# Reordering the work ahead of the first expert slots and moving the gate1 multiply of the output weights from VectorE to GpSimd

## Chip, cores and metric

The kernel runs on one core of one Trainium2 chip. The metric is the device time of one execution in microseconds. Engines are named as in the profile: PE (TensorE; PEld its weight loads), DVE (VectorE), ACT (ScalarE), POOL (GpSimd), SP (SyncE). A timeline row gives start, duration, engine, line of the kernel, operation, output<-inputs and count; the bracket behind it is the engine's idle time before it and what ended that.

## What is computed

One decoder layer on a sequence of 1024 tokens of width 1024, all in float32. A mixer (causal pooling beside spatial gating) and then a product-key retrieval network over 16384 experts of one neuron each:

```python
mod = silu(c) @ w_ada + b_ada                      # shift1, scale1, gate1, shift2, scale2, gate2
h = rms_norm(x, g_norm1) * (1 + scale1) + shift1
a, u, v = split(h @ w_in)
mixed = concat([pool_mixer(a), spatial_gating(u, v)])
x = x + gate1 * (mixed @ w_out)
h = rms_norm(x, g_norm2) * (1 + scale2) + shift2
q = (h @ w_query).reshape(T, 8 heads, 2, 128)
s_top, i_top = top_k(q . sub_keys, 16)             # two sides of 128 keys for each head
best, sel = top_k(all 16 x 16 sums, 16); gate = softmax(best)
act = gelu(expert_down[idx] . h)                   # 16 experts a head, 128 a token
x = x + gate2 * sum(gate * act * expert_up[idx])
out = rms_norm(x, g_final)
```

## The kernel before

The tokens are cut into 8 tiles of 128. Each tile has 128 slots, 1024 in all; a slot is one expert for each of the 128 partitions. A partition holds a quarter of a token's work, so that a slot fetches 128 rows of 8 KB (down and up row of an expert), 1 MB, with one indirect DMA from POOL's queue into a ring of 7 buffers. In slot g DVE takes the dot product of the row with the token's h (`dot`, L1560), ACT applies Gelu and the gate and builds a diagonal (`expert_weight`, L1130 to L1137), and PE adds the up rows, weighted by that diagonal, into PSUM (`add_expert`, L900). PE's product counts up `s_free`, which lets POOL issue the gather of slot g + 7. A slot of late tiles has 9 buffers.

The work of the eight tiles is laid out by hand: every engine has its own instruction list, made by Python loops, and waits only on semaphores, so an instruction stands behind everything ahead of it on its engine. Between the slot's own steps each engine's loop over `TABLE` carries out steps of four other jobs at fixed slot numbers:

- the mixer of the next tile, 35 steps n, in slot MIX_AT[tile] + n (`mixer`): norm and transposes (0 to 4), projection to v in four steps of two matmuls 128x512 (PROJECT_V, 5 to 8), to a (9 to 12), to u (13 to 20), pooling and gating, the output projection (25 to 32), the residual (34). Tile 1 has its steps below MIX_HEAD ahead of the slots.
- the queries and scores of the next "turn" (two heads of a tile: 4 sides, each a query of 8 matmuls, an ACT copy, a score matmul, an ACT copy), at SIDE_AT. Each side's weights come by a load on SP's queue into three buffers.
- the routing of a turn on DVE, 19 steps from ROUTE_AT (`route_step`): top 16 of each side, of the sums, their indices, softmax weights (the exponential is ACT's, `exp_logits`), then `move_choices` on PE (L889), which spreads the chosen rows and gates over the partitions, and `place_choices` on DVE (L1552), which writes the rows that POOL's gathers read. POOL waits for it at the first slot of each routing (`s_placed`). Routings 0 and 1 are the two heads of turn 0 (slots 0 to 31, four of the one and four of the other in turn), routing 2 is turn 1 (slots 32 to 63).
- spreading h over the partitions (`spread_first_h2`, PE L725, ACT copies L1103), rows of shift2 and scale2, and others. These share one PSUM bank ("wide"), whose uses are put in a fixed order by `wide_bank_uses`; a `moved` use takes the first free pair of slots from ROUTE_AT + 19.

Ahead of the slots stands the head: the adaLN sums of the six parts of w_ada (2 x 2 MB each), the whole mixer of tile 0, the norm of its result (L1328 residual, L1385 to L1412 statistics and scales), routings 0 and 1, part of tile 1's mixer and the four queries of turn 1. Tile 0's mixer multiplies its result by gate1 itself (L1325); for the later tiles w_out is multiplied by gate1 once, in place, in four parts of 128x2048 (`scale_w_out`, L1269, on DVE in slots 3, 6, 9 and 12). SP's queue issues all plain loads in order, those of x for tile 1 (L514) and then of the last w_ada part, GATE2, behind the residual of tile 0. GATE2's sums on PE (L679) must be done before routing 0's last step, since that overwrites their other operand. POOL's list is two memsets, a wait on GATE2's sums, and the gathers.

## Time and profile before

| | us |
|---|---|
| median of 3 runs | 2828.95 (2825.89 to 2829.47) |
| the profiled execution | 2833.91 |
| its span | 2832.1 |
| mean granted TensorE clock | 0.712 |

| | busy us | share | instructions |
|---|---|---|---|
| PE | 1938.6 | 68% | 13316 |
| DVE | 1894.8 | 67% | 4714 |
| ACT | 1210.7 | 43% | 3867 |
| POOL | 1123.1 | 40% | 1030 |

A busy share is a mean over the whole span; the table of stretches further down shows the parts. A DMA share near 1 means that the 16 DMA engines have packets all the time. GB/s is what they moved.

### The profile page before, as it was taken

What the parts mean: (1) busy time and instruction counts of PE and PEld (TensorE: products, weight loads), DVE (VectorE), ACT (ScalarE), POOL (GpSimd) and SP (SyncE); (2) the same over time, 40 slices, a digit from 0 to 9 for tenths busy, and PEclk for the clock granted to TensorE, in tenths of its full rate; (3) what the DMA queues carried; (4) which work ended last, traced back from release to release, by engine and by line L of the source; (5) the groups of instructions that cost most, each with busy time, mean ns of one, the idle gap of its engine ahead of it and who ended that gap; (6) DMA issues with size and microseconds to landing.
All of it is one profiled execution on the core that took longest, in us unless ns stands there. A gap on an engine that the chain in (4) does not pass through costs nothing.

```text
span 2832.1 us, 38640 instructions
## 1 busy us (share of the span) xinstructions
PE 1938.6 (68%) x13316; PEld 893.8 (32%) x13316; DVE 1894.8 (67%) x4714; ACT 1210.7 (43%) x3867; POOL 1123.1 (40%) x1030
## 2 busy tenths in 40 slices
PE   5898898888886566666656666665666666665553
PEld 4555354444442222232323222221322323221110
DVE  5686776785766567677666757677676756676454
ACT  1245445454453344454444434444343544344333
POOL 0044334344443254444444444444444444344342
PEclk9998898899886566665666667665766666576555
DMA  9899999999999999999999999999999999999997
GB/s 404 339 373 403 396 413 417 409 420 420 420 401 397 416 422 421 421 421 421 421 421 421 421 421 419 416 421 421 417 415 421 419 421 416 421 415 421 421 420 294
DMA packets 169221, 1162.38 MB, mean 410 GB/s; under 512 B 19009, under 2 KB 25665, under 8 KB 35778
## 3 DMA queue, kind: packets, MB, share of 16 engines
q0 software_dynamic: 147456, 1073.81, 91.9%
q1 hardware_dynamic: 21570, 86.11, 7.7%
q8 instruction: 106, 1.74, 0.2%
q14 instruction: 89, 0.73, 0.1%
HBM read 1151.97 MB, written 7.86 MB: 410 GB/s over the span
## 4 chain that ended last, share of the span: by engine, by line
DMA 54%; PE 22%; DVE 11%; ACT 6%; issue 3%; SPq 3%; POOL 0%; another core or an unknown queue 0%; DVEq 0%; POOLq 0%; ACTq 0%
DMA work<-experts,expert_rows 41%; DMA more_ring<-experts,expert_rows 8%; PE ps_sum L900 7%; DVE work L1560 5%; PE ps_small L866 5%; PE ps_m L815 4%; DMA work<-w_ada 2%; PE ps_m L759 2%; DMA weights<-experts,expert_rows 1%; ACT diag L1137 1%; ACT weight L1132 1%; DMA vn_u<-x_scratch 1%; PE ps_wide L841 1%; SPq L613 1%; PE ps_m L770 1%
## 5 line engine op out<-in xcount | busy, mean ns | idle before, releaser
L650 POOL DMA_INDIRECT work<-experts,expert_rows x818 | 899.0, 1099 | 1378.7 <-PE ps_sum L900 1225.8
L1560 DVE CUSTOM_DVE_ANT_0 work<-work 128x1024 f32<-128x1024 f32 x818 | 997.5, 1221 | 589.3 <-DMA work<-experts,expert_rows 573.4
L900 PE MATMUL ps_sum<-work,diag 128*32 128x256 f32 x6544 | 717.5, 523 | 674.7 <-ACT diag L1137 653.6
L1130 ACT ACTIVATE act_out<-act_in 128x1 f32<-128x1 f32 x1024 | 207.4, 203 | 1162.8 <-DVE act_in L1560 1141.9
L900 PEld LDWEIGHTS ps_sum<-work,diag 128*32 128x32 f32 x6544 | 150.1, 126 | 1146.5 <-ACT diag L1137 1052.1
L1137 ACT ACTIVATE diag<-const,weight 128x32 f32<-128x32 f32 x1024 | 329.2, 321 | 33.5
L1132 ACT ACTIVATE weight<-gate,act_out 128x1 f32<-128x1 f32 x1024 | 301.6, 295 | 33.3
L866 PE MATMUL ps_small<-h_t,weights 128*128 128x128 f32 x1344 | 291.2, 384 | 0.0
L866 PEld LDWEIGHTS ps_small<-h_t,weights 128*128 128x128 f32 x1344 | 249.3, 278 | 125.7 <-issue 120.4
L1560 DVE CUSTOM_DVE_ANT_0 more_ring<-more_ring,work 128x1024 f32<-128x1024 f32 x122 | 149.1, 1222 | 91.5 <-DMA more_ring<-experts,expert_rows 90.4
L650 POOL DMA_INDIRECT more_ring<-experts,expert_rows x122 | 134.8, 1105 | 180.3 <-PE ps_sum L900 175.5
L841 PE MATMUL ps_wide<-h_cur,const 32*128 32x512 f32 x244 | 191.0, 872 | 0.0
L900 PE MATMUL ps_sum<-more_ring,diag 128*32 128x256 f32 x976 | 108.1, 527 | 85.0 <-ACT diag L1137 84.1
L1560 DVE CUSTOM_DVE_ANT_0 weights<-weights,work 128x1024 f32<-128x1024 f32 x84 | 102.7, 1222 | 67.8 <-DMA weights<-experts,expert_rows 66.3
L1103 ACT COPY work<-ps_wide 128x512 f32<-128x512 f32 x144 | 83.5, 580 | 130.4 <-PE ps_wide L841 107.3
L900 PE MATMUL ps_sum<-weights,diag 128*32 128x256 f32 x672 | 80.1, 564 | 82.3 <-ACT diag L1137 80.2
L650 POOL DMA_INDIRECT weights<-experts,expert_rows x84 | 88.2, 1050 | 120.3 <-PE ps_sum L900 119.1
L815 PE MATMUL ps_m<-weights,h_buf 128*128 128x512 f32 x256 | 124.8, 615 | 0.0
L1110 ACT COPY q_t<-ps_small 128x128 f32<-128x128 f32 x124 | 32.3, 261 | 123.5 <-PE ps_small L866 122.8
L1560 DVE DVE_READ_ACCUMULATOR2_ANT act_in<- 128x1 f32 x1024 | 83.6, 82 | 0.0
L1130 ACT ACT_TABLE_LOAD x59 | 75.7, 1283 | 2.0 <-DVE act_in L1560 0.9
L900 PEld LDWEIGHTS ps_sum<-more_ring,diag 128*32 128x32 f32 x976 | 22.5, 126 | 151.1 <-ACT diag L1137 139.5
(200 smaller groups left out, 1991.1 us busy)
## 6 DMA issues: line engine op xcount, KB each, us to landing
work<-w_ada SPq DMA_DIRECT2D x12, 2048.0 KB, 23.6
work<-sides SPq DMA_DIRECT2D x26, 576.0 KB, 8.4
work<-experts,expert_rows POOLq DMA_INDIRECT x818
weights<-sides SPq DMA_DIRECT2D x16, 576.0 KB
more_sides<-sides SPq DMA_DIRECT2D x12, 576.0 KB
weights<-w_in SPq DMA_DIRECT2D x3, 2048.0 KB, 17.2
x_buf<-x SPq DMA_DIRECT2D x8, 512.0 KB, 11.4
weights<-w_out SPq DMA_DIRECT2D x2, 2048.0 KB, 37.5
```

What stands on the lines that cost most here:

```text
L650: nc.gpsimd.indirect_dma_start(ring[x.ring], None, experts, bass.IndirectOffsetOnAxis(ap=rows_flat[:, x.column:x.column + 1], axis=0),).th ...
L759: last = nc.tensor.matmul(ps_v[:, :], h_t[:, k, :], w_in_sb[:, 0, k, :], start=(k == 0), stop=(k == KC - 1))
L815: last = nc.tensor.matmul(ps_out[half], mixed_t[:, k, :], w_out_sb[:, k, half * HALF:(half + 1) * HALF], start=(part == 0 and i == 0), sto ...
L841: nc.tensor.matmul(ps_wide[:, :], quads[quarter(group), :], source[quarter(group), half * HALF:(half + 1) * HALF], start=True, stop=True). ...
L866: last = nc.tensor.matmul(ps_query(n), w_q[:, k, :], h2_t[:, k, :], start=(k == 0), stop=(k == KC - 1))
L900: last = nc.tensor.matmul(ps_sum[quarter(c), x.group, :], diag[:, x.ring, :], ring[x.ring][:, D + c * QCOLS:D + (c + 1) * QCOLS], start=x. ...
L1103: nc.scalar.copy(h2_spread[k % 2][:, half * HALF:(half + 1) * HALF], ps_wide[:, :]).then_inc(s_wide_sb, 1)
L1110: nc.scalar.copy(q_t[:, n % 2, :], ps_query(n)).then_inc(s_q_sb, 1)
L1130: nc.scalar.activation(act_out[:, s:s + 1], act_in[:, s:s + 1], ACT.Gelu).then_inc(s_gelu, 1)
L1132: nc.scalar.mul(weight[:, s:s + 1], gate_flat[:, x.column:x.column + 1], act_out[:, s:s + 1]).then_inc(s_weight, 1)
L1137: nc.scalar.mul(diag[:, x.ring, :], quad_rows, weight[:, s:s + 1]).then_inc(s_diag, 1)
L1560: nc.vector.tensor_tensor_reduce(down, down, h2_spread[x.segment % 2], 1.0, 0.0, ALU.mult, ALU.add, act_in[:, x.g % TURN:x.g % TURN + 1]). ...
```

## The change

Four things are done.

1. The order of PE's and ACT's lists ahead of the slots. On PE: the first side of turn 1 stands between the two halves of the first spread; the second placement's `move_choices(1)` goes behind the second side, ahead of its score; of tile 1's mixer only steps 0 to 5 stay in the head (MIX_HEAD 6 in place of 9), and the fourth side of turn 1 goes to slots 0 to 4 (SIDE_AT[0]). On ACT: `exp_logits(1)` goes right behind the second spread copy; the copies of h, queries and scores are interleaved to match.
2. Slot numbers: tile 1's mixer steps come three slots later, those of tiles 2 to 4 two slots later; the routing of turn 1 starts in slot 5 in place of 2.
3. `scale_w_out` is taken from DVE's list. POOL's list has the same four products, between its memsets and its first gather, behind waits for tile 0's output sums (`s_o`) and gate1 (`s_mod`).
4. SP's list ahead of the slots ends one side load earlier; the loop issues that load at slot 4.

```diff
--- before.py
+++ after.py
@@ -58,10 +58,10 @@
 PROJECT_A, PROJECT_U, SPATIAL, COPY_A, COPY_U = 9, 13, 14, 13, 21
 WINDOWS, MEANS, GATED, POOLED, COPY_Y, PROJECT_OUT, RESIDUAL = 21, 22, 23, 24, 25, 25, 34
 MIX_STEPS = RESIDUAL + 1
-MIX_HEAD = PROJECT_A
-MIX_AT = {1: -MIX_HEAD, 2: 31, 3: 70, 4: 109, 5: 150, 6: 190, 7: 230}
-
-SCALE_W_SLOTS = (3, 6, 9, 12)
+MIX_HEAD = PROJECT_V + 1
+MIX_AT = {1: -MIX_HEAD, 2: 33, 3: 72, 4: 111, 5: 150, 6: 190, 7: 230}
+
+SCALE_W_PARTS = 4
 
 
 STATS2, ROOT2, NORM2, TURN_H2, COPY_H2 = 0, 1, 2, 3, 4
@@ -85,7 +85,7 @@
 EXP_SLOT, MOVE_SLOT = 11, 19
 SIDES_BEFORE = (20, 15, 10, 5)
 SIDES_CLOSE = (17, 13, 9, 5)
-ROUTE_AT = [None, 2, 28, 50, 74, 98]
+ROUTE_AT = [None, 5, 28, 50, 74, 98]
 for _t in range(1, TILES):
     ROUTE_AT += [SLOTS * _t + s for s in (2, 28, 68, 94)][:2 if _t == TILES - 1 else 4]
 
@@ -174,6 +174,7 @@
 SIDE_AT = {(ROUTE_AT[e] - (SIDES_CLOSE if e == HELD_FROM else SIDES_BEFORE)[b]): (e, b)
            for e in range(2, TURNS) for b in range(4)}
 assert len(SIDE_AT) == 4 * (TURNS - 2)
+SIDE_AT[0] = (1, 3)
 
 
 def streamed(e):
@@ -536,7 +537,7 @@
                 if t >= 2:
                     sp.wait_ge(s_out, 64 * (t - 1))
                 else:
-                    sp.wait_ge(s_scaled_w, len(SCALE_W_SLOTS))
+                    sp.wait_ge(s_scaled_w, SCALE_W_PARTS)
                     sp.wait_ge(s_x1_gated, 1)
                 sp.dma_start(h2_next[:, :], x1_dram[t]).then_inc(s_x1n, 16)
 
@@ -596,7 +597,7 @@
                 sp.dma_start(ring[FIRST_SIDES[b]][:, 0:SIDE], sides[b]).then_inc(s_side0, 16)
             load_ada(GATE2, 0)
             load_ada(GATE2, 1)
-            for n in range(2, 6 + SIDE_BUFS):
+            for n in range(2, 5 + SIDE_BUFS):
                 load_side(*FIRST_USE[n])
 
             for g in range(TILES * SLOTS):
@@ -635,6 +636,12 @@
         def _(pool):
             nc.gpsimd.memset(a_t[:, :, 0:HALO], 0.0).then_inc(s_halo0, 1)
             nc.gpsimd.memset(gate1[:, :], 0.0).then_inc(s_zero, 1)
+            pool.wait_ge(s_o, 1)
+            pool.wait_ge(s_mod, 2)
+            for n in range(SCALE_W_PARTS):
+                part = w_out_sb[:, 2 * n:2 * n + 2, :]
+                nc.gpsimd.tensor_tensor(part, part, gate1[:, :].unsqueeze(1).to_broadcast([P, 2, D]),
+                                        ALU.mult).then_inc(s_scaled_w, 1)
             pool.wait_ge(s_gate2_ps, 2)
             for x in TABLE:
                 if x.opens:
@@ -807,7 +814,7 @@
                             for i in range(2):
                                 pe.wait_ge(s_w_out[i], 16)
                         if t == 1:
-                            pe.wait_ge(s_scaled_w, len(SCALE_W_SLOTS))
+                            pe.wait_ge(s_scaled_w, SCALE_W_PARTS)
                     if n == PROJECT_OUT + 4:
                         pe.wait_ge(s_ymix, t + 1)
                     for i in (2 * pair, 2 * pair + 1):
@@ -969,19 +976,18 @@
             for half in range(2):
                 quarter_sums(GATE2, half, ps_gate2, s_gate2_ps)
             move_choices(0)
-            for half in range(2):
-                spread_first_h2(0, half)
+            spread_first_h2(0, 0)
+            side(1, 0)
+            spread_first_h2(0, 1)
             mixer(TURN_H, 1)
-            for b in range(2):
-                side(1, b)
-                scores(1, b)
+            scores(1, 0)
+            side(1, 1)
+            move_choices(1)
+            scores(1, 1)
             for n in range(TURN_H + 1, MIX_HEAD):
                 mixer(n, 1)
-                if n == PROJECT_V + 1:
-                    move_choices(1)
-            for b in range(2, 4):
-                side(1, b)
-                scores(1, b)
+            side(1, 2)
+            scores(1, 2)
 
             for x in TABLE:
                 for tile, n in mixer_steps(x.g):
@@ -1169,15 +1175,17 @@
                 copy_score(0, b)
             mixer(SCALE_H, 1)
             exp_logits(0)
-            for half in range(2):
-                copy_spread(0, half)
-            for n in range(SCALE_H + 1, MIX_HEAD):
-                mixer(n, 1)
-            for b in range(4):
-                if b == 2:
-                    exp_logits(1)
-                copy_query(1, b)
-                copy_score(1, b)
+            copy_spread(0, 0)
+            copy_query(1, 0)
+            copy_spread(0, 1)
+            exp_logits(1)
+            copy_score(1, 0)
+            mixer(COPY_H, 1)
+            copy_query(1, 1)
+            mixer(COPY_H + 1, 1)
+            copy_score(1, 1)
+            copy_query(1, 2)
+            copy_score(1, 2)
 
             for x in TABLE:
                 expert_weight(x)
@@ -1261,13 +1269,6 @@
                                                           scalar=ln_b[:, g:g + 1], in1=sgu_bias[:, g, :],
                                                           op0=ALU.mult, op1=ALU.add)
                 last.then_inc(s_bias, 1)
-
-            def scale_w_out(n):
-                dve.wait_ge(s_o, 1)
-                dve.wait_ge(s_mod, 2)
-                part = w_out_sb[:, 2 * n:2 * n + 2, :]
-                nc.vector.tensor_tensor(part, part, gate1[:, :].unsqueeze(1).to_broadcast([P, 2, D]),
-                                        ALU.mult).then_inc(s_scaled_w, 1)
 
             def gate2_rows():
                 dve.wait_ge(s_gate2_ps, 2)
@@ -1638,8 +1639,6 @@
                     normalize(x.tile - 1)
                 if x.g in FIRST_H2_SLOTS:
                     first_h2(FIRST_H2_SLOTS.index(x.g))
-                if x.g in SCALE_W_SLOTS:
-                    scale_w_out(SCALE_W_SLOTS.index(x.g))
                 for tile, n in mixer_steps(x.g):
                     mixer(n, tile)
                 if x.tile + 1 < TILES and x.s == PREP_AT[x.tile] + STATS2:
```

## Rows read from the trace of the kernel before

**Rows 1.** The page, DMA queues: packets, MB, share of 16 engines; gathers.

```profile
q0 software_dynamic: 147456, 1073.81, 91.9%
```

**Rows 2.** Stretches: busy PE, PEld, DVE, ACT, POOL; granted clock, DMA share, GB/s.

```profile
106.00:114.00 8.00, 5.21 (x72) 2.75 (x69) 5.07 (x30) 0.20 (x1) 2.42 (x3) 0.53 0.30 95
124.00:132.00 8.00, 7.64 (x30) 3.50 (x29) 2.59 (x10) 0.65 (x3) 2.02 (x3) 1.00 0.58 179
132.00:146.00 14.00, 11.98 (x126) 10.14 (x125) 9.97 (x29) 7.56 (x17) 3.51 (x3) 1.00 0.85 324
146.00:160.00 14.00, 14.00 (x151) 10.13 (x150) 14.00 (x40) 6.74 (x22) 6.64 (x6) 1.00 0.96 349
160.00:2800.00 2640.00, 1809.45 (x12366) 806.97 (x12364) 1778.83 (x4454) 1158.42 (x3733) 1104.37 (x1009) 0.70 1.01 417
```

**Rows 3.** Timeline of POOL: memset of gate1, gathers of slots 0, 4 and 7.

```profile
0.83 0.95 POOL L637 MEMSET h_next<- 128x1024 f32 x1
110.97 1.08 POOL L650 DMA_INDIRECT work<-experts,expert_rows  x1 [109.19 <-DVE expert_rows L1552]
...
129.38 0.94 POOL L650 DMA_INDIRECT work<-experts,expert_rows  x1 [13.60 <-DVE expert_rows L1552]
...
142.01 1.78 POOL L650 DMA_INDIRECT work<-experts,expert_rows  x1 [9.21 <-PE ps_sum L900]
```

**Rows 4.** Timeline of DVE, 106 to 110 us: gates of head 0, their spread.

```profile
106.76 0.17 DVE L1528 TENSOR_TENSOR chosen<-expd,sums 128x16 f32<-128x16 f32 x1
109.06 0.36 DVE L1540 TENSOR_TENSOR chosen_own<-chosen,const 128x64 f32<-128x64 f32 x2 [2.13 <-PE ps_sum L679]
```

**Rows 5.** Timeline of ACT, then DVE, 125 to 129 us: routing 1.

```profile
125.39 0.22 ACT L1121 ACTIVATE expd<-logits 128x16 f32<-128x16 f32 x1
...
125.71 0.17 DVE L1524 TENSOR_REDUCE sums<-expd 128x1 f32<-128x16 f32 x1 [6.76 <-ACT expd L1121]
...
128.93 0.17 DVE L1552 CAST expert_rows<-ps_wide 128x16 uint32<-128x16 f32 x1 [2.25 <-PE ps_wide L889]
```

**Rows 6.** Timeline of ACT, then PE, 138 to 142 us: slot 0.

```profile
138.47 0.27 ACT L1116 COPY wide<-ps_small 128x128 f32<-128x128 f32 x1 [0.58 <-PE ps_small L879]
...
141.08 0.64 PE L900 MATMUL ps_sum<-work,diag 128*32 128x256 f32 x8 [0.86 <-ACT diag L1137]
```

**Rows 7.** Timeline of PE: a query, four V matmuls, the first A group.

```profile
122.32 2.02 PE L866 MATMUL ps_small<-h_t,work 128*128 128x128 f32 x16 [0.45 <-ACT wide L1116]
...
125.02 3.60 PE L759 MATMUL ps_m<-weights,h_t 128*128 128x512 f32 x8
...
138.27 1.95 PE L770 MATMUL ps_m<-h_t,weights 128*128 128x128 f32 x16
```

**Rows 8.** Timeline of DVE: the first of the four w_out products; all four.

```profile
140.69 2.28 DVE L1269 TENSOR_TENSOR weights<-weights,h_next 128x2048 f32<-128x2048 f32 x1
...
L1269 DVE TENSOR_TENSOR weights<-weights,h_next x4: 2280/2282/2284, 140.7 to 167.6; 128x2048 f32<-128x2048 f32 x4
```

**Rows 9.** Timeline of DVE, 82 to 98 us: from tile 0's residual to routing 0.

```profile
82.30 1.29 DVE L1325 TENSOR_TENSOR h_buf<-ps_m,h_next 128x512 f32<-128x512 f32 x2 [1.01 <-PE ps_m L815]
83.62 1.22 DVE L1328 TENSOR_TENSOR h_buf<-h_buf,x_buf 128x1024 f32<-128x1024 f32 x1
...
86.45 0.22 DVE L1390 SCALAR_TENSOR_TENSOR stat<-h_mean_var 128x1 f32<-128x1 f32 x1
...
90.86 0.17 DVE L1412 TENSOR_TENSOR mod_cols<-mod_cols,cols 128x8 f32<-128x8 f32 x1
...
97.42 0.49 DVE L1455 MAX8 top_s<-wide 128x8 f32<-128x128 f32 x2 [3.99 <-ACT wide L1116]
```

**Rows 10.** POOL, PE and DVE, 211 to 227 us: gather 32, slot 29, dot product 32.

```profile
211.90 1.27 POOL L650 DMA_INDIRECT work<-experts,expert_rows  x1 [1.02 <-PE ps_sum L900]
...
216.86 0.64 PE L900 MATMUL ps_sum<-work,diag 128*32 128x256 f32 x8 [0.94 <-ACT diag L1137]
...
226.34 1.22 DVE L1560 CUSTOM_DVE_ANT_0 work<-work 128x1024 f32<-128x1024 f32 x1 [2.13 <-DMA work<-experts,expert_rows]
```

## The prediction, made before the changed kernel ran

> **What bounds the kernel now.** I read the page first. The gathers of expert rows move 1074 MB, and their packets alone take 91.9% of the 16 DMA engines' span [rows 1]. Next the busy time by stretch: from 160 to 2800 us the DMA share is 1.01 at 417 GB/s while PE, DVE and POOL all have room, so after 160 us the end moves only if DMA idle time is added or removed. What a head edit can win is the idle DMA time ahead of 160 us. Against 417 GB/s the stretches lack: 106 to 114 (1 - 95/417) x 8 = 6.2 us; 124 to 132 (1 - 179/417) x 8 = 4.6; 132 to 146 (1 - 324/417) x 14 = 3.1; 146 to 160 (1 - 349/417) x 14 = 2.3 [rows 2]. The sum behind 124 us is 10.0 us.
>
> The timelines say what each gap waits for. The first gather starts at 110.97, the fifth, the first of the second head, at 129.38, the eighth, which needs slot 0 freed, at 142.01 [rows 3]. 106 to 114 is the wait for the first placement: DVE has the gates of head 0 ready at 106.76 + 0.17 = 106.93 and spreads them at 109.06, when GATE2's sums are done on PE, so 2.1 us of slack [rows 4]. 124 to 132 is the second placement: its exponential is the ACT instruction at 125.39, since ACT reaches it only behind two queries and two scores; DVE had done all else and sat 6.76 us for it, and placed at 128.93 [rows 5]. 132 to 146 is slot 0: ACT copies the last score of the head at 138.47 and only then loads the table for slot 0, whose product is on PE at 141.08 [rows 6].
>
> **The change part by part.**
>
> Order on PE and ACT. Durations are those of before, only their order changes. PE: spread half 0 as now, the first query of turn 1 (2.0 us at full clock [rows 7]; up to 4 at the lower level, which the granted 0.53 of 106 to 114 shows [rows 2]), spread half 1, transposes, score. ACT then does the exponential right behind the second spread copy, at about 119.5 in place of 125.39. Behind it DVE needs 0.9 us, PE finishes a query (2.0) and moves the choices: placement at 123 to 124.5, against 128.93. So the fifth gather goes 4.5 to 6 us earlier, about when the first four have landed (1.05 MB at 417 GB/s is 2.5 us; four from about 113 end at 123), and side loads, now at 120 to 124, cover the start. The 4.6 us gap goes.
>
> In front of slot 0's product PE no longer has two steps of the V projection (1.8 us each), group A's first 16 matmul records (1.95 us) and the fourth query with its score (2.0 + 0.5 us) [rows 7]. Slot 0's product comes at about 130 to 133 against 141.08, and the eighth gather with it, while gathers five to seven need the queue until about 134. The 3.1 us go too. What is moved is issued again in slots 0 to 3: 8 us of PE work. Its cover is the rows already landed, but a slot took PE (216.86 - 141.08)/29 = 2.6 us as it is [rows 6, 10] against 2.5 of a gather, so some idleness comes back, between 0 and 3 us; I take 1.5.
>
> The output weights. Four DVE instructions of 2.28 us leave slots 3 to 12 [rows 8], where DVE is busy 14.0 of 14.0 us [rows 2]: 9.1 us off an engine that was full there. This lets DVE follow the product's pace; its worth is inside the 2.3 us of 146 to 160. POOL takes four multiplies instead. Its start is allowed at 82.3, when PE's output sums end [rows 9], and its next duty is the gather at 110.97, so POOL itself hides them while one costs under (110.97 - 82.3)/4 = 7.2 us. No row shows a POOL multiply. A memset of 1024 columns takes 0.95 us there [rows 3]: one pass of 2048 is 1.9 us, and two reads and a write in turn are three passes, 5.7 us. I take two, 3.8 us, as a multiply reads twice per word written. Nothing waits for its end but the gathers, tile 1's output projection (slot 19) and a load in slot 37.
>
> The Trainium skill (GPSIMD Engine Reference, 3.1) has 4.5 us for a two-input operation of this size on GpSimd, against 2.3 on VectorE, which the 2.28 of [rows 8] agrees with; four would end near 101, also in cover.
>
> Contention. The gather at 142.01 took 1.78 us against 0.94 for a free one: the DVE multiply from 140.69 ended at 142.97 and the gather ended 0.82 later [rows 3, 8]. So a POOL instruction stands while DVE runs with two SBUF inputs. No row shows the other direction, a long POOL instruction ahead of such a DVE one; the DVE multiply itself took 2.28 in all four places, gathers beside it or not [rows 8]. Bounds: nothing, or DVE waits for the whole multiply. In the second case I walk the head [rows 9] with 3.8 us: the first multiply runs 82.4 to 86.2 and the residual's addition (two SBUF inputs, 83.62) waits for it, +2.5; the second 87.4 to 91.2, and the small square of the mean (86.45) waits, +4.7 in all. The third ends at 95.2, and then it hangs on who is first: DVE's product for the second norm's scale (90.86, now 95.6), leaving +4.7, or the fourth multiply, making +8.3. The first routing, at 97.42 now, has 2.1 us of slack, so the first gather slips 2.6 or 6.2 us; I take the middle, 4.5. SP's queue slips with it: the load of x and behind it both halves of GATE2 wait for the residual's sum. By 5.7 us a multiply the same walk gives +9.8, by 1.9 nothing.
>
> The Trainium skill speaks against the change here: SBUF — State Buffer, "Who interferes with whom", has a VectorE instruction with two SBUF inputs and a GpSimd one that reads SBUF exclude each other for a whole instruction, the first to issue winning. The trace agrees in the one direction that it shows. With its 4.5 us the walk gives +4.9, so a time of 2827.3; without the rule, 2822.4.
>
> Routing of turn 1. It goes from slots 2 to 20 to slots 5 to 23, and the move of its choices asks for slot 24. Two uses of the wide bank hold 25 to 28, so by the kernel's own table it lands in slot 29 in place of 21, and DVE places in slot 30. The gather of slot 32 and all behind it on POOL's queue wait for that. Now it goes at 211.90, after slot 25, and its dot product waits for the row until 226.34, a queue of 14.4 us; slot 29's product is at 216.86 [rows 10]. After the change PE reaches slot 0 some 10 us earlier with 8 us more to do, less some of its waits, so slot 29 comes at 212 to 215, and the gather a placement later, at 213 to 216. In an empty queue the row needs about 2 us of way (my estimate: 0.94 of issue, and the gap of 124 to 132 goes on past that of 129.38 [rows 2, 3]) and 2.5 of data: 217.5 to 220.5, which is 6 to 9 us ahead of 226.34 though it is issued later. Rows 30 and 31 (5.0 us), x1's store and x's load (1 MB, 2.5 us) are queued meanwhile, so the hole is 0 to 5 us; I take 2.
>
> Tiles 2 to 4 mix two slots later, and a side load of turn 2 is issued from SP's loop in place of in front of it, with nothing that SP waits for between: nothing.
>
> Sum: -10.0 + 1.5 + 2 = -6.5 for the order, +4.5 for contention: -2.0. The profiled execution took 2833.9 (span 2832.1), 5.0 above the median 2828.95; 2831.9 by it, and 2827.0 from the median, as the gap is the same for both kernels.
>
> **The rivals.**
>
> No contention: DVE isn't held. For it: no DVE row was ever stretched. Against: the gathers are, by DVE. 2828.95 - 6.5 = 2822.4.
>
> A dear multiply: 7 us each and exclusive. First to 89.4, second 90.6 to 97.6, third to 104.8, fourth 105 to 112, and DVE's two diagonal products behind it (1.2 us each, as the addition of the same width [rows 9]) hold the first routing to 114.4: the first gather slips about 15 us, hence 2837.4. It decides for slower by 0.2% from about 6.3 us a multiply; the memset speaks for less.
>
> The order brings nothing: PE sets the pace of slots 3 to 26, so what is won in front is lost in an idle queue before slot 32. For it: PE is busy 14.0 of 14.0 us in 146 to 160. Against: the 14.4 us of queue at the gather of slot 32. With light contention, 2829.
>
> **How the numbers follow.** Forecast 2827.0, chance 0.47 (its own range 2823 to 2832.5); no contention 0.33; dear multiply 0.1; nothing won 0.1. The range reaches down to -10.0 with nothing given back, 2819.0, and up to 9.8 - 6.5 = +3.3 plus a hole a little larger than taken, 2833.5; it leaves out the dear multiply and tails. 0.2% is 5.7 us, about what a measurement of this kernel can tell from no change. Faster: most of the second case (0.27) and the lower end of the first (0.06), 0.33; slower 0.12; same 0.55.
>
> **What would show it.** POOL rows of the multiplies of about 4 us from 82.4. The addition at 83.62 and the square of the mean later by 2 to 5 us if contention is real, at their old times if not; the first gather at 111 or at 113.5 to 117. From first to fifth gather 18.4 us now, 12 to 14 then; from first to eighth 31.0 now, 20 to 23 then. DMA share near 1 from the fifth gather on, and a dip ahead of slot 32. Wrong would be the whole if the share in 160 to 2800 were well under 1 afterwards.

## The result and the profile after

| | us |
|---|---|
| before, median of 5 runs | 2828.95 (2825.89 to 2832.24) |
| after, median of 5 runs | 2840.89 (2839.71 to 2841.83) |
| ratio after/before | 1.0049, 95% interval 1.0038 to 1.0060 |
| profiled execution of after | 2841.78, span 2840.0 |

The change makes the kernel slower, by 11.9 us in the medians and 13.9 by the ratio; 2827.0 was forecast, with 2833.5 as the upper end.

The busy time by stretch of the changed kernel (columns as in [rows 2]):

```profile
114.00:124.00 10.00, 7.15 (x113) 4.66 (x113) 9.02 (x44) 3.98 (x7) 1.49 (x2) 0.90 0.07 26
124.00:132.00 8.00, 7.10 (x82) 6.35 (x82) 7.05 (x30) 3.80 (x12) 2.43 (x3) 0.92 1.00 372
132.00:146.00 14.00, 12.72 (x97) 7.64 (x97) 4.98 (x9) 6.25 (x20) 5.77 (x5) 1.00 1.01 419
146.00:160.00 14.00, 14.00 (x148) 10.43 (x147) 11.11 (x37) 7.76 (x20) 4.22 (x5) 1.00 1.02 420
200.00:220.00 20.00, 20.00 (x112) 7.92 (x110) 7.58 (x14) 5.78 (x24) 6.42 (x5) 1.00 0.84 340
220.00:240.00 20.00, 11.57 (x84) 5.29 (x76) 13.67 (x52) 7.77 (x24) 9.41 (x9) 0.69 0.88 321
160.00:2800.00 2640.00, 1841.56 (x12387) 821.57 (x12385) 1777.91 (x4468) 1160.11 (x3726) 1094.88 (x1006) 0.69 1.01 415
```

The three stretches behind 124 us that lacked 10 us of traffic [rows 2] are full from 132 on (419, 420 GB/s). New gaps stand at 200 to 240 (340 and 321 GB/s), and the largest is 114 to 124, where the queues moved 26 GB/s, since the first gather had not landed. The long stretch behind 160 hides such gaps from its share, which still reads 1.01. Its rate doesn't: 415 GB/s in place of 417 is about 13 us of 2640, give or take 6 by rounding.

Timelines of POOL and then DVE in the changed kernel (start, duration, engine, line, operation, count, idle before and what ended it):

```profile
82.54 18.92 POOL L643 TENSOR_TENSOR weights<-weights,h_next 128x2048 f32<-128x2048 f32 x4 [80.76 <-PE ps_m L822]
...
122.20 1.11 POOL L657 DMA_INDIRECT work<-experts,expert_rows  x1 [20.75 <-DVE expert_rows L1553]
...
132.08 0.94 POOL L657 DMA_INDIRECT work<-experts,expert_rows  x1 [5.04 <-DVE expert_rows L1553]
...
139.90 0.93 POOL L657 DMA_INDIRECT work<-experts,expert_rows  x1 [3.30 <-PE ps_sum L907]
...
225.71 0.94 POOL L657 DMA_INDIRECT work<-experts,expert_rows  x1 [11.17 <-DVE expert_rows L1553]
```

```profile
83.81 4.36 DVE L1329 TENSOR_TENSOR h_buf<-h_buf,x_buf 128x1024 f32<-128x1024 f32 x1
...
89.77 2.77 DVE L1391 SCALAR_TENSOR_TENSOR stat<-h_mean_var 128x1 f32<-128x1 f32 x1
...
97.44 4.04 DVE L1413 TENSOR_TENSOR mod_cols<-mod_cols,cols 128x8 f32<-128x8 f32 x1
...
110.76 0.49 DVE L1456 MAX8 top_s<-wide 128x8 f32<-128x128 f32 x2 [6.88 <-ACT wide L1122]
```

POOL's four products fill 82.54 to 101.46, 4.73 us each; the shortest took 4.49. The three DVE instructions with two SBUF operands that fall in that time, 1.22, 0.22 and 0.17 us long before [rows 9], show 4.36, 2.77 and 4.04: their time in the record includes the wait. Routing 0 begins at 110.76 against 97.42, the first gather goes at 122.20 against 110.97 [rows 3], 11.2 us late. From there on the order works better than forecast: fifth gather 9.9 us behind the first (18.4 before), eighth 17.7 (31.0 before). By 160 us the kernel has moved only 0.3 MB less than before did, 0.7 us of traffic, where it was 9.9 us behind at 124. Then POOL stands 11.17 us before gather 32.

The query matmuls of routing 0 on PE are the second part of the slip, first in the kernel before and then in the changed one:

```profile
91.73 3.81 PE L714 MATMUL ps_m<-h_t,work 128*128 128x128 f32 x32 [1.18 <-ACT h_t L1090]
```

```profile
94.00:102.00 8.00, 2.82 (x12) 2.42 (x12) 4.77 (x4) 0.68 (x3) 7.46 (x2) 0.50 1.03 438
...
102.00:109.00 7.00, 6.70 (x32) 6.54 (x32) 1.88 (x2) 2.78 (x10) 0.00 (x0) 0.55 0.67 283
...
102.18 6.70 PE L721 MATMUL ps_m<-h_t,work 128*128 128x128 f32 x32 [5.05 <-ACT h_t L1096]
```

In 94 to 102 PE was busy 2.82 of 8 us and its granted clock was 0.50, the 1.2 GHz level; while it did the queries, 102 to 109, it was 0.55.

### The profile page after: what moved, and what is told of

Same layout as the page of the kernel before. It is cut to its first block, busy times and chain, and to the rows that moved or that the text cites. A ratio compares the mean times of both kernels' runs of the same rounds, so it can differ in the third digit from the quotient of the medians.

```text
span 2840.0 us, 38640 instructions
## 1 busy us (share of the span) xinstructions
PE 1968.5 (69%) x13316; PEld 905.5 (32%) x13316; DVE 1898.0 (67%) x4710; ACT 1213.9 (43%) x3868; POOL 1133.6 (40%) x1034
## 4 chain that ended last, share of the span: by engine, by line
DMA 53%; PE 25%; DVE 12%; ACT 6%; issue 3%; SPq 2%; POOL 0%; DVEq 0%; POOLq 0%; ACTq 0%
DMA work<-experts,expert_rows 39%; DMA more_ring<-experts,expert_rows 11%; PE ps_sum L907 7%; DVE work L1561 4%; PE ps_small L873 4%; PE ps_m L822 4%; DMA weights<-experts,expert_rows 2%; PE ps_wide L848 2%; PE ps_m L766 2%; PE ps_m L777 2%; PE ps_m L786 1%; ACT weight L1138 1%; ACT diag L1143 1%; DMA vn_u<-x_scratch 1%; SPq L614 1%
## 5 line engine op out<-in xcount | busy, mean ns | idle before, releaser
L907 PE MATMUL ps_sum<-work,diag 128*32 128x256 f32 x6544 | 730.9, 532 | 651.3 <-ACT diag L1143 642.4
L873 PE MATMUL ps_small<-h_t,weights 128*128 128x128 f32 x1344 | 298.2, 391 | 0.0
L873 PEld LDWEIGHTS ps_small<-h_t,weights 128*128 128x128 f32 x1344 | 255.5, 284 | 130.0 <-issue 124.3
L848 PEld LDWEIGHTS ps_wide<-h_cur,const 32*128 32x128 f32 x244 | 48.7, 247 | 74.6 <-issue 74.6
```

The lines of the kernel that those rows point to most:

```text
L848: nc.tensor.matmul(ps_wide[:, :], quads[quarter(group), :], source[quarter(group), half * HALF:(half + 1) * HALF], start=True, stop=True). ...
L873: last = nc.tensor.matmul(ps_query(n), w_q[:, k, :], h2_t[:, k, :], start=(k == 0), stop=(k == KC - 1))
L907: last = nc.tensor.matmul(ps_sum[quarter(c), x.group, :], diag[:, x.ring, :], ring[x.ring][:, D + c * QCOLS:D + (c + 1) * QCOLS], start=x. ...
```

## The experiments

Theory after the result: the slip of the first gather is contention between POOL and DVE plus a slower PE behind it, and costs its length at the end; the order wins in the head what it gives back by slot 40. Rivals: the slip comes from the later loads; the order's gain is real and something else takes it. Where gathers are named by number, 0 is the first. The kernel before, run beside each group of experiments, had medians from 2826.4 to 2830.6, so the ratios are to be compared and not the times.

### One part alone

**e1_order**: the changed kernel with the products back on DVE in slots 3, 6, 9, 12.

```diff
+SCALE_W_SLOTS = (3, 6, 9, 12)
-            for n in range(SCALE_W_PARTS):
-                part = w_out_sb[:, 2 * n:2 * n + 2, :]
-                nc.gpsimd.tensor_tensor(part, part, gate1[:, :].unsqueeze(1).to_broadcast([P, 2, D]),
-                                        ALU.mult).then_inc(s_scaled_w, 1)
...
+                if x.g in SCALE_W_SLOTS:
+                    scale_w_out(SCALE_W_SLOTS.index(x.g))
```

> The changed order and slot numbers alone; the output weights are multiplied on VectorE in slots 3, 6, 9 and 12 as before. Theory A (the whole first slip of 11.2 us is VectorE held by the POOL multiply): the addition of the residual takes 1.2 us again, the first gather starts near 111.0, and the time is that of the changed kernel less about 11: 2829.5 (2826 to 2832). Rival B (the new order costs by itself in the head): the first gather stays later than 113 and the time above 2834. Both expect the pause before the gather of slot 32 to stay.

Measured: 2831.79, ratio 1.0004 (0.9995 to 1.0013).

**e2_multiply**: the kernel before with the four products on POOL, nothing else.

```diff
             nc.gpsimd.memset(gate1[:, :], 0.0).then_inc(s_zero, 1)
+            pool.wait_ge(s_o, 1)
+            pool.wait_ge(s_mod, 2)
+            for n in range(SCALE_W_PARTS):
...
-                if x.g in SCALE_W_SLOTS:
-                    scale_w_out(SCALE_W_SLOTS.index(x.g))
```

> The kernel before with the POOL multiply alone: order and slot numbers of before. Theory A: the rows of the changed kernel's head come back, addition 4.4 us, square of the mean 2.8, scale of the second norm 4.0, first gather at about 122.2, and 2828.95 + 11.2 = 2840 less at most 2 that VectorE gains in slots 3 to 12: 2838 to 2840. Rival B: the multiply costs under 5 us, below 2834.

Measured: 2841.55, ratio 1.0036 (1.0022 to 1.0050). POOL and DVE of e2, the same rows as in the changed kernel:

```profile
82.28 18.91 POOL L642 TENSOR_TENSOR weights<-weights,h_next 128x2048 f32<-128x2048 f32 x4 [80.50 <-PE ps_m L821]
...
121.21 1.11 POOL L656 DMA_INDIRECT work<-experts,expert_rows  x1 [20.02 <-DVE expert_rows L1551]
```

```profile
83.55 4.35 DVE L1327 TENSOR_TENSOR h_buf<-h_buf,x_buf 128x1024 f32<-128x1024 f32 x1
...
89.50 2.77 DVE L1389 SCALAR_TENSOR_TENSOR stat<-h_mean_var 128x1 f32<-128x1 f32 x1
...
97.17 4.04 DVE L1411 TENSOR_TENSOR mod_cols<-mod_cols,cols 128x8 f32<-128x8 f32 x1
```

So the products alone give 1.0036 of the 1.0049, and the order alone 1.0004. Two such parts sum to 1.0040, which the interval of the whole (1.0038 to 1.0060) holds. The order is worth nothing that these runs resolve.

**e3_move** and **e4_order_move**: the changed kernel, and e1, with the move of turn 1's choices in the wide bank's slot 23 in place of 29, which takes away the pause before gather 32.

```diff
-        g = ROUTE_AT[e] + MOVE_SLOT
+        g = ROUTE_AT[e] + (18 if e == 1 else MOVE_SLOT)
```

> The changed kernel with one number changed: the move of turn 1's choices takes the wide bank in slot 23 in place of 29, so that VectorE places them in slot 24 and POOL can issue the gather of slot 32 when slot 25 is free. Theory C (the pause of 11 us in POOL's queue before slot 32 costs 6 us of DMA time): 2840.9 - 6 = 2835 (2833 to 2837), and a DMA share of 1.0 in 200 to 240. Rival D (PE's pace in slots 3 to 26 empties the queue, the placement only falls into that): no more than 2 us less, 2839 or above.

> Both: the changed order, the multiply on VectorE in slots 3 to 12, and the move in slot 23. Theory A with C: 2828.95 - 10 + 4 = 2823 (2821 to 2826), faster than the kernel before. Rival D: like the order alone, 2828 to 2831, and the order has nothing to give.

Measured: e3 2839.01, ratio 1.0031 (1.0020 to 1.0042); e4 2829.05, ratio 0.9994 (0.9985 to 1.0003). Gather 32 with and without the pause, POOL of e1 and then of e4:

```profile
216.01 0.94 POOL L652 DMA_INDIRECT work<-experts,expert_rows  x1 [12.04 <-DVE expert_rows L1555]
```

```profile
208.29 0.94 POOL L652 DMA_INDIRECT work<-experts,expert_rows  x1 [2.07 <-PE ps_sum L902]
```

Gather 32 goes 7.7 us earlier and the end 2.7 us; the queue covers the rest. From after to e3 it is 0.0018 of the ratio, 5 us, with intervals that allow 1 to 10. Rival D, that the pause matters little, held in both runs. The hole of 2 in the prediction, with its 0 to 5, was right in size.

### How POOL's products hold DVE

**e8_short_parts**: e2 with eight products of 128x1024 in place of four of 128x2048.

```diff
-SCALE_W_PARTS = 4
+SCALE_W_PARTS = 8
-                part = w_out_sb[:, 2 * n:2 * n + 2, :]
-                nc.gpsimd.tensor_tensor(part, part, gate1[:, :].unsqueeze(1).to_broadcast([P, 2, D]),
-                                        ALU.mult).then_inc(s_scaled_w, 1)
+                part = w_out_sb[:, n, :]
+                nc.gpsimd.tensor_tensor(part, part, gate1[:, :], ALU.mult).then_inc(s_scaled_w, 1)
```

With 1024 columns to a product gate1 is no longer repeated within it, a second small difference to e2.

> The kernel before with the POOL multiply in the head in 8 parts of 1024 columns in place of 4 of 2048. If VectorE is held for the whole of one POOL instruction and gets in between two, each wait is at most half as long: the addition under 3 us, square of the mean and scale under 2.4 each, first gather at 113 to 117, and 2832 to 2836. If VectorE is held until POOL's list of products is done, or the sharing is by the word, nothing changes: 2840 to 2842.

Measured: 2829.72, ratio 1.0012 (1.0003 to 1.0021). POOL and DVE of e8:

```profile
80.73 21.79 POOL L642 TENSOR_TENSOR weights<-weights,h_next 128x1024 f32<-128x1024 f32 x8 [78.95 <-PE ps_m L820]
...
111.68 1.11 POOL L655 DMA_INDIRECT work<-experts,expert_rows  x1 [9.16 <-DVE expert_rows L1550]
```

```profile
82.38 2.09 DVE L1326 TENSOR_TENSOR h_buf<-h_buf,x_buf 128x1024 f32<-128x1024 f32 x1
...
86.07 0.62 DVE L1388 SCALAR_TENSOR_TENSOR stat<-h_mean_var 128x1 f32<-128x1 f32 x1
...
91.87 1.76 DVE L1410 TENSOR_TENSOR mod_cols<-mod_cols,cols 128x8 f32<-128x8 f32 x1
93.67 3.33 DVE L1416 TENSOR_TENSOR shift<-const,mod_cols 128x1024 f32<-128x1024 f32 x1
96.93 3.37 DVE L1416 TENSOR_TENSOR scale<-const,mod_cols 128x1024 f32<-128x1024 f32 x1
```

POOL multiplies for longer (21.79 us in all), yet the three rows fall to 2.09, 0.62 and 1.76. DVE waits for one instruction of POOL, not for its whole stretch. When it is already waiting at the end of a product, it goes ahead of POOL's next one, whose record holds the wait in turn: 5.48 us for the second product of e2 against 4.49 for the shortest, and in e8 3.32 to 3.34 for three of the eight against 2.34. The two diagonal products of 1.2 us now show 3.33 and 3.37, since POOL is still at it. The first gather is at 111.68, 9.5 us ahead of e2, and the result is better than the 113 us and 2832 expected.

**e11_after_short**: the changed kernel with both edits, eight short products and the move in slot 23.

> The changed kernel with the GpSimd products in eight parts of 128x1024 instead of four of 128x2048, and turn 1's move six slots earlier. Theory (each VectorE instruction is held to the end of one GpSimd product, so halving the products cuts the hold of 4.36, 2.77 and 4.04 us to about a third; the first gather's slip of 11.2 us falls to 1 to 3): first gather at 111.5 to 114, time 2829 to 2831 against 2839.0 with whole parts. Rival (the slip is a matter of the whole time that GpSimd multiplies, 19 us, or of the later x load): first gather at 119 to 122, time 2836 to 2839.

Measured: 2828.59, ratio 1.0006 (0.9997 to 1.0015); first gather 110.82. e3, the same with long products, had 1.0031 and 121.71. The order and the move are the same in both, so the shorter products alone take 0.0025 off the time and 10.9 us off the first gather.

The rival of the later loads needs more than that, since with short products the residual's sum, and so the loads behind it, come earlier too. The changed kernel's own trace settles it; PE's sums of GATE2 and then DVE's spread of the gates of head 0:

```profile
115.06 3.66 PE L686 MATMUL ps_sum<-work,chosen_own 128*32 128x256 f32 x64
...
120.32 0.36 DVE L1541 TENSOR_TENSOR chosen_own<-chosen,const 128x64 f32<-128x64 f32 x2
```

PE takes both halves of GATE2 in one go without waiting for a load, has them done at 118.72, and DVE, which waited 2.13 us for them before [rows 4], reaches its spread later than that and doesn't wait. The loads set nothing here, so the rival falls.

**e5_vector_head**: e4 with the four products on DVE, two in the head and two in slots 1 and 2.

```diff
-SCALE_W_SLOTS = (3, 6, 9, 12)
+SCALE_W_SLOTS = (1, 2)
             mod2_diagonals()
+            scale_w_out(0)
+            scale_w_out(1)
```

> The changed order with the move in slot 23, and the four products of the output weights on VectorE where it stands idle in that kernel: two behind the diagonals of the head (4.0 us idle at 93, 2.2 us of slack behind the first routing), two in slots 1 and 2 (5.7 us idle ahead of the v statistics). Theory: VectorE no longer holds up slots 3 to 12, PE gets some 2 to 4 us further by slot 12, and the time falls 1 to 4 us below the kernel with the products in slots 3 to 12: 2825 to 2828. Rival: PE alone sets the pace there, within 1 us of it.

Measured: 2826.07, ratio 0.9999 (0.9990 to 1.0008). Against e4 (0.9994) that resolves nothing: no gain from the place of the products among DVE's work shows, where 1 to 4 us were expected.

### PE behind its idle time

**f1_multiply_pe_fed**: e2 with five more matmuls 128x512 between the spread of scale2 and the first queries.

```diff
+            for k in range(5):
+                nc.tensor.matmul(ps_m3[:, :], ident, w_in_sb[:, 0, k, :], start=True, stop=True)
             pe.wait_ge(s_ymix, 1)
             first_queries()
```

> The kernel before with the four GpSimd products ahead of its first gather (as in the run with the multiply alone), and five more matmuls 128x512 on TensorE between the spread of scale2 and the first queries, where it otherwise waits 5.05 us for ACT; their sums are overwritten by the queries. Theory (the 32 first query matmuls take 5.98 to 6.70 us in place of 3.81 because the engine had been idle and its granted clock was low): with the engine fed they take 3.8 to 4.5 us, the first gather comes 1.5 to 3 us earlier than at 121.0 of the multiply alone, and the time falls from 1.0036 to 1.0027 to 1.0031. Rival (they are slow because of GpSimd's products or the memory beside them): they take 6 us or more again, first gather and time unchanged or later by up to 2 us.

PE of f1, the added matmuls and the first queries, and behind them the stretch 102 to 109 of e2 and then of f1 (columns as in [rows 2]):

```profile
96.70 5.95 PE L967 MATMUL ps_m<-weights,const 128*128 128x512 f32 x10
102.48 3.73 PE L720 MATMUL ps_m<-h_t,work 128*128 128x128 f32 x32
```

```profile
102.00:109.00 7.00, 6.38 (x35) 6.05 (x35) 1.60 (x2) 2.97 (x10) 0.00 (x0) 0.68 0.63 265
```

```profile
102.00:109.00 7.00, 6.38 (x51) 5.75 (x50) 2.53 (x8) 4.23 (x13) 0.00 (x0) 1.00 0.78 301
```

The queries took 3.73 us in place of 5.98, at a clock of 1.00 in place of 0.68, with POOL's products as before. So the 2.9 us in the changed kernel (6.70 against 3.81) are PE at its lower level after idling. The first gather came 1.7 us earlier (119.54 against 121.21). The time, 2837.33, ratio 1.0042 (1.0029 to 1.0056), doesn't resolve 1.7 us; what this term is worth at the end stays open.

### What the order had to win

**e9_before_again** and **e9b_before_again**: the kernel before, unchanged.

> The kernel before, unchanged, once more. Theory (the profiled execution that the prediction was worked from was not typical: TensorE's granted clock was 0.53 and 0.69 in 106:114 and 114:124, and the gap of 4.6 us in 124:132 stood behind it): clock near 1.00 in 106:124, slot 0's product near 136 to 138 instead of 141.08, DMA traffic in 124:132 over 300 GB/s instead of 179, span near 2827. Rival (the gap belongs to the order of the head, as the prediction had it): traffic in 124:132 again near 180 GB/s whatever the clock, slot 0 near 141.

> The same as the run beside it, a second execution of the kernel before, so that the clock and the gap are seen twice. Theory: whichever of the two has a low clock in 106:124 has the gap in 124:132, and the one without hasn't. Rival: both have the gap whatever the clock.

Measured: 2826.09 and 2826.64, spans 2824.3 and 2824.8, against 2832.1 of the execution that the prediction was read from. Stretches of e9 (columns as in [rows 2]):

```profile
106.00:114.00 8.00, 6.37 (x100) 5.09 (x93) 6.62 (x35) 2.59 (x7) 3.89 (x4) 0.79 0.55 196
...
124.00:132.00 8.00, 7.10 (x41) 5.05 (x39) 4.11 (x8) 0.59 (x3) 2.50 (x3) 1.00 0.85 303
132.00:146.00 14.00, 12.89 (x167) 10.80 (x168) 12.51 (x44) 10.07 (x25) 4.79 (x4) 1.00 0.87 332
146.00:160.00 14.00, 14.00 (x147) 9.89 (x146) 14.00 (x30) 5.76 (x22) 7.52 (x7) 1.00 0.97 372
```

The clock in 106 to 114 was 0.79 (0.53 in [rows 2]) and 1.00 in 114 to 124 (0.69 then). That it makes the difference fits the two executions but no run changed it alone. The gap of 124 to 132 is (1 - 303/417) x 8 = 2.2 us in place of 4.6, and gather 7, which needs slot 0 freed, goes at 136.32 in place of 142.01 [rows 3]. Summed as in the prediction, the three stretches behind 124 lack 2.2 + 2.9 + 1.5 = 6.6 us, and 7.1 in e9b, not 10.0. The traces also say where that execution lost its time: by 160 it has moved 5.9 us of traffic less than e9, and its span is 7.8 longer.

**e6_order_less_pe** and its control **e7_before_less_pe**: e4 and the kernel before with half of tile 1's output projection (8 of 16 matmuls 128x512, steps 25 to 32 of its mixer) left out.

```diff
-                    for i in (2 * pair, 2 * pair + 1):
+                    for i in ((3 * pair,) if t == 1 else (2 * pair, 2 * pair + 1)):
```

> The changed order, products on VectorE, move in slot 23, and in tile 1's output projection every second matmul left out (8 of 16, 7 us of PE work, so tile 1's result isn't the reference's). Rival D of the first series (PE's pace in slots 3 to 31 eats the 9 us that the head won): the time falls by 4 to 7 us, to 2822 to 2825, and the DMA share in 180 to 220 is 1. If PE isn't the limit there, 2828 to 2830 as with all matmuls.

> The kernel before with the same 8 matmuls of tile 1's output projection left out: the control. Its DMA queue was long in slots 3 to 31, with 2.4 us missing in 200 to 220. PE's pace theory: it gains that and no more, 1 to 3 us (2827 to 2829). If leaving out PE work gives 5 us or more here too, then the gain of the run beside it says nothing of the order.

Measured: 2824.87, ratio 0.9992 (0.9983 to 1.0001), and 2824.24, ratio 0.9994 (0.9985 to 1.0003). That is 0.0002 below e4 and 0.0006 below the kernel before, neither clear of noise. The traffic further down says more.

The starts of some gathers, from POOL's timelines:

| gather | e9 (before) | e4 | e11 | f2 | f4 |
|---|---|---|---|---|---|
| 0 | 108.6 | 110.6 | 110.8 | 109.6 | 112.5 |
| 7 | 136.3 | 128.8 | 129.2 | 127.3 | 131.2 |
| 16 | 159.2 | 157.4 | 156.6 | 157.6 | 156.7 |
| 28 | 197.3 | 195.8 | 192.8 | 193.6 | 191.4 |
| 44 | 240.7 | 241.2 | 240.7 | 241.8 | 239.8 |
| 72 | 319.3 | 326.4 | 325.9 | 325.1 | 325.1 |

e4 leads by 7.5 us at gather 7 and by 1.8 at gather 16; the nine gathers between take 28.6 us in e4 and 22.9 in e9, which is 2.54 us each, the pace of the queue itself.

The start of a gather isn't traffic, though: a later one costs nothing while the queue is full. What a kernel has moved by a time says what it has won. The lead over e9 in MB by then, put as us at 417 GB/s (the differences of a stretch from 0 in the profile's GB/s give the same), is:

| lead in us at | e9b | e7 (before) | f3 (before) | e4 | e6 | e11 | f2 | f4 |
|---|---|---|---|---|---|---|---|---|
| 124 | -1.1 | -1.8 | -2.6 | -2.0 | -2.6 | -2.4 | -0.6 | -4.2 |
| 160 | -1.5 | -1.5 | -0.1 | 3.5 | 3.5 | 4.1 | 3.3 | 2.7 |
| 200 | -0.2 | 0.8 | -0.9 | 1.6 | 3.6 | 4.0 | 3.2 | 5.0 |
| 240 | -1.3 | 1.7 | -1.7 | 0.5 | 4.5 | 3.2 | 2.6 | 4.7 |
| 340 | -0.9 | 2.1 | -2.6 | -2.9 | 1.0 | -2.9 | -2.4 | -1.5 |

The first three have the order and slots of before, the rest the new ones; e9b and e11 ran in e9's group, and the others may carry the level of their own; e6, e7, f2, f3 and f4 leave matmuls out. The new order wins 4 to 7 us between 124 and 160. e4 gives 3.0 back by 240, e6 with less work for PE nothing. But between 240 and 340 each of the nine kernels with the new slots loses 2.9 to 6.2 us against e9 (e10, with some slots of before, 6.9), and the seven other traces with the old slots lie between 0.4 won and 1.9 lost. That is where the order's lead ends, whatever was saved before it.

**f2_order_half_au**, **f3_before_half_au**: e4 and the kernel before with every second matmul of tile 1's projections to a and u left out. **f4_short_half_au**: e11 with the same.

```diff
-                    for k in range(KC):
+                    step = 2 if t == 1 else 1
+                    for k in range(0, KC, step):
```

> The order without the GpSimd products and with turn 1's move earlier, and of tile 1's projections to a and u only every second matmul (32 of 64 left out; they stand in slots 3 to 14). Theory (in slots 0 to 14 TensorE sets the pace, so that the lead of 7.5 us at the eighth gather over the kernel before is down to 1.7 at the seventeenth): the nine slots from the eighth to the seventeenth gather take 24 to 26 us in place of 28.6, and the lead at the seventeenth is 4 to 6 us; the time 2826 to 2828 if that lead is kept to slot 40, 2829 if it is lost again at slots 24 to 32. Rival (the pace there is set by VectorE or by the gathers' own landing): 28 to 29 us again, time unchanged.

> The kernel before with the same 32 matmuls of tile 1 left out, as control. Theory (its gathers from the eighth to the seventeenth take 22.9 us, already 2.54 us for each slot at over 410 GB/s in the record once they run, so TensorE isn't in their way): 22.5 to 23 us again, and the time lower by at most 1 us. Rival (TensorE sets the pace in this kernel too): 20 to 22 us, time lower by 2 us or more.

> The changed kernel with the products in eight short parts on GpSimd and turn 1's move earlier (as e11), and of tile 1's projections to a and u only every second matmul (32 of 64 left out). Either of the two alone left the pace of slots 8 to 16 as it was: without VectorE's products the eighth to the seventeenth gather took 27.4 us with TensorE busy for all of 146:160, and with half of TensorE's matmuls 30.3 us with VectorE busy for all of it. Theory (two engines, both full, set that pace together): with both relieved it takes 22.5 to 25.5 us and the lead over the kernel before at the seventeenth gather is 4 us or more; the time 2825 to 2828. Rival (a chain of waits between the three engines, not their work, sets it): 27 us or more again.

Measured: f2 2827.81, ratio 1.0004 (0.9995 to 1.0013); f3 2826.94, ratio 0.9998 (0.9989 to 1.0007); f4 2825.30, ratio 0.9982 (0.9973 to 0.9992). The stretch 146 to 160 of e11, of f2 and of f4, in this order:

```profile
146.00:160.00 14.00, 14.00 (x150) 10.76 (x149) 14.00 (x46) 7.00 (x23) 5.36 (x5) 1.00 1.01 411
```

```profile
146.00:160.00 14.00, 11.18 (x102) 7.77 (x102) 14.00 (x42) 5.45 (x18) 3.41 (x4) 0.76 0.86 334
```

```profile
146.00:160.00 14.00, 12.89 (x140) 8.87 (x136) 14.00 (x53) 6.70 (x21) 7.10 (x6) 1.00 1.01 420
```

My theory for f2, that PE alone sets the pace of the gathers, fell: with half of its matmuls gathers 7 to 16 took 30.3 us, PE had room (11.18 of 14) and DVE had none. Without DVE's products but with all matmuls (e11) they took 27.4, and PE was busy throughout. With both relieved (f4) they took 25.5, at 420 GB/s, but gather 16 started no earlier than in e11, and its lead over e9 was 2.5 us where 4 was expected. The ratios say more: f4's is clear of e11's and of f2's, while leaving the matmuls out won nothing without the relief of DVE (f2) and nothing in the control f3. So both engines stand in the way, PE with tile 1's projections and DVE with turn 1's routing in the same slots. How much is each one's isn't resolved: by traffic, e4 loses 1.9 us of its lead from 160 to 200, e11 and f2 0.1 each, and f4 gains 2.3, while the two unchanged executions part by 1.3 there. The control f3 took 21.6 us for the gathers in place of 22.9, and its time did not change.

**e10_mix_back**: e4 with the mixers of tiles 2 to 4 back in the slots of the kernel before.

```diff
-MIX_AT = {1: -MIX_HEAD, 2: 33, 3: 72, 4: 111, 5: 150, 6: 190, 7: 230}
+MIX_AT = {1: -MIX_HEAD, 2: 31, 3: 70, 4: 109, 5: 150, 6: 190, 7: 230}
```

> The change's order without the GpSimd products and with turn 1's move six slots earlier, and in addition the mixers of tiles 2 to 4 back in the slots of the kernel before (31, 70, 109 for 33, 72, 111). Theory (part of what the order wins in the head is given back in 300:320, where the shifted mixer of tile 2 stands on TensorE's path: 5.3 us of missing traffic there against 2.7 before): the loss in 300:320 goes to about 2.7 and the time falls by 2 to 3 us, to a ratio of 0.998 to 0.999 against before. Rival (the ring of seven buffers makes every early gain be given back at the next stretch where TensorE is late, wherever the mixer stands): the loss comes at another place, ratio 0.9994 to 1.000 as without this edit.

Measured: 2832.12, ratio 1.0019 (1.0010 to 1.0028), slower than e4. Stretches 220 to 240 and 300 to 320 of e10, and what ACT and DVE stand for in the first:

```profile
220.00:240.00 20.00, 11.00 (x54) 4.93 (x54) 12.19 (x37) 12.52 (x32) 4.85 (x5) 0.57 0.88 354
...
300.00:320.00 20.00, 20.00 (x99) 8.12 (x98) 16.39 (x40) 8.65 (x24) 6.66 (x7) 1.00 0.97 362
```

```profile
225.02 1.06 ACT L1031 ACTIVATE h_buf<-x_buf 128x1024 f32<-128x1024 f32 x1 [7.08 <-DMA x_buf<-x]
...
227.81 0.16 DVE L1342 RECIPROCAL stat<-stat 128x1 f32<-128x1 f32 x1 [8.61 <-ACT stat L1033]
```

The loss of 300 to 320 is gone as expected (362 GB/s; e4 had 309), but tile 2's first step now needs x from a load that SP issues at 210.40, behind tile 1's residual, with gathers queued ahead of it. ACT waits 7.08 us for it and DVE 8.61 for ACT, and more is lost there than won later: its lead over e9 goes from 2.7 us at 200 to -0.8 at 240 and -6.8 at 300. The rival, that the loss only changes its place, held, and the loss grew. By this trace the two slots of shift are the price of tile 1's mixer coming three slots later.

## Why the prediction was wrong

- **Contention, forecast +4.5 at the first gather, measured +11.2 (e2 against the three executions of before: 10.2 to 12.6).** This term is 6.7 us short and the -6.5 for the order, which came to about nothing, is nearly all of the rest of the 13.9 us between 2827.0 and 2840.9. The mechanism was right: DVE is held for the whole POOL instruction. Three sizes failed. A product is 4.7 us in the record, not 3.8; "I take two [passes]" from a memset was the step. Then, "it hangs on who is first": I took the middle of a fork that has no middle, and my own walk had the third product end at 95.2 and DVE's product ready at 95.6, when POOL's next would already be at it. So it was: the fourth began at 96.97 and DVE was ready at 97.44, and the scale product ended at 101.48 in place of 91.03, +10.4, where the walk had +4.7 or +8.3. Last, nothing in the sum asked what PE does meanwhile: it idled, fell to 0.50 and took 2.9 us more for the queries. It also set the fork: the sums ahead of DVE's product took PE 2.82 us in place of 1.53, and 1.3 us earlier that product would have been waiting when the third one ended, where by e2 and e8 it goes first. That is an estimate from these rows; no run tests it. 10.4 + 2.9 - 2.1 of slack = 11.2. The walk for 5.7 us a product gave +9.8, so a product of 4.7 was already close to the rival that I priced at 0.10; its point of decision, "about 6.3 us", was too high by that fork and by the clock.
- **The two rules of the Trainium skill** came out better than my rows: GPSIMD Engine Reference, 3.1, has 4.5 us for a two-input operation of this size (4.49 here undisturbed, 4.73 with DVE's turns included), and SBUF — State Buffer, "Who interferes with whom", has the two engines exclude each other for a whole instruction (4.36, 2.77 and 4.04 here for instructions of 1.22, 0.22 and 0.17). The walk with 4.5 that gave +4.9 took the kind branch of the fork; the other gives +8.9, my estimate from the same rows, against 10.4 - 2.1 = 8.3 measured ahead of the queries.
- **Order in the head, -10.0: right for what it was read from, wrong as a worth.** The gaps went as said (fifth gather 9.9 us behind the first where 12 to 14 was forecast, eighth 17.7 where 20 to 23 was). But the size was that of one execution with PE at 0.53 and 0.69 in 106 to 124; others have 6.6 to 7.1, and by traffic e4 and e11 win 5.5 and 6.5 on e9 between 124 and 160. "The gap is the same for both kernels" was the step: the 5.0 us between that execution and the median were partly the very gap that I counted as winnable.
- **Idleness that comes back while PE catches up, +1.5: measured 3.0** by traffic, from e4's lead of 3.5 at 160 to 0.5 at 240. The starts of gathers 7 to 16 lie 5.7 us further apart (28.6 against 22.9), but part of that the full queue covers. I had seen PE at 14.0 of 14.0 and took comfort in DVE's relief; f4 shows that both engines had to be relieved.
- **Hole before gather 32, +2: right** within its 0 to 5 (2.7 from e1 to e4; 5 from after to e3, by the intervals 1 to 10).
- **"Tiles 2 to 4 mix two slots later ...: nothing" was wrong.** The new slots lose 2.9 to 6.2 us between 240 and 340 in every trace that has them, e4 3.4, which takes back what was left of the gain. In 300 to 320 e4 lacks (1 - 309/417) x 20 = 5.2 us and e9 (1 - 340/417) x 20 = 3.7, e4's line first:

```profile
300.00:320.00 20.00, 20.00 (x94) 7.97 (x94) 13.29 (x30) 10.02 (x32) 5.20 (x5) 0.90 0.85 309
```

```profile
300.00:320.00 20.00, 20.00 (x121) 9.05 (x121) 12.44 (x28) 9.36 (x27) 9.16 (x8) 1.00 0.95 340
```

  e10 shows that the shift can't simply be taken back. Which of the moved slots costs this stays open.
- **The rivals.** "The order brings nothing" was right in its result (1.0004, 0.9994), but not in its place: the lead ends behind slot 44, with DVE beside PE ahead of that; "no contention" is ruled out by e2. The outcome is these two cases together, order 0 and contention beyond the middle, while I had given them chances as if only one could come.
- **The share of 160 to 2800** was named as the sign that would show the whole wrong. It stayed at 1.01 (415 GB/s for 417) with two gaps in it of 3.7 and 4.6 us: the stretch was too long for its share to show them.

No version measured here beats the kernel before with all of its work done: the best are e4 (0.9994) and e5 (0.9999). f4, 0.9982, leaves matmuls out.

## What to carry to other kernels

Before work is given to an idle engine, list the instructions of the other engine that share its access to SBUF and fall in that time: each is held for up to one whole instruction, however short it is itself, so where work must go there, it goes in short pieces. Walk the forks to the end and price each, and then ask what the third engine's clock does while it waits. A gap that is to be won is looked up in several executions, and a lead in the head is followed by what the queues have moved at each time, not by when a gather starts, to where it ends.

## What the runs showed of the hardware

- A DVE instruction with two SBUF operands stands while POOL multiplies: 0.17 us became 4.04, 0.22 became 2.77. With products of half the width they were 1.76 and 0.62. One with a single operand stood too: the cast of 128x32 at 100.62 in e11 took 1.78 us, to the end of POOL's last product, and 0.18 in the changed kernel.
- DVE, waiting when a POOL product ends, goes ahead of the next: that one's record is 5.47 us in place of 4.49 (it starts at 87.05, and DVE's addition, 1.22 us long alone, ends at 88.17).
- A POOL product 128x2048 f32 takes 4.7 us, one of 128x1024 2.7 (21.79/8) with DVE taking turns, and 4.49 and 2.34 at the least; the same product on DVE takes 2.28.
- PE, granted 0.50 of its clock in 94 to 102 with 6.48 and 5.05 us without work, and 0.55 in 102 to 109, took 6.70 us for 32 matmuls that take 3.73 to 3.81 at 1.00. In f1, with five matmuls 128x512 in the second idle time, the clock was 1.00 when they ran.
- The granted clock of a stretch differs between executions of one program (0.53, 0.79 and 0.81 in 106 to 114 of the kernel before), and the first gather (110.97, 108.58, 109.57) and the span (2832.1, 2824.3, 2824.8) differ too. In what order these hang together, no run shows.
